# A pair's softmax inverses on one trip: one reciprocal, one transfer out, one back, and the multiplication moved in VectorE's order

## The chip, the cores and the metric

The kernel runs on one core of one Trainium2 chip. The metric is the device time of one execution in microseconds. Engines are named as in the profile: PE is TensorE (PEld its weight loads), DVE is VectorE, ACT is ScalarE, POOL is GpSimd, SP is SyncE. An engine with a `q` behind it (ACTq, SPq) is its queue as it issues a DMA.

## The reference, cut to what matters

The program computes two small transformer blocks over 512 tokens of width 1024. Two of its attentions are softmax attentions: `chunk_causal_softmax_attention` of the first block ("MLA", 8 heads) and `fox_attention` of the second ("fox", 16 heads, with a decay added to the scores).

```python
z = jnp.einsum("bhqd,bshd->bhqs", q_blk, k).astype(jnp.float32) * scale
p = jax.nn.softmax(jnp.where(allowed, z, -jnp.inf), axis=-1)
return jnp.einsum("bhqs,bshd->bhqd", p.astype(v.dtype), v)
```

The softmax divides by the sum of a query's exponentials. In MLA the output is also multiplied by a gate before its projection.

## The kernel before

All matrix products are of float32 operands split into a high and a low part, so each tile is three matmuls (lines 1171 to 1173) or, in attention, two or three (L1520, L1557). ScalarE writes the high part, VectorE subtracts it for the low part (`low`, L2704).

Both softmax attentions go over pairs of heads (4 in MLA, 8 in fox). Each pair has eight steps `s` = 0 to 7: four blocks of 128 queries of its first head, four of its second. The products of another unit of work (a projection) run beside it in eight shares. On every engine the order of a pair is written out by hand, as a string of a letter and a number, and the engines meet by semaphores alone: an instruction that waits holds everything behind it on its engine. Orders differ by kind and place: `_MLA` and `_MLA_LAST`; `_FOX` for pairs 0 to 5, `_NEAR` for pair 6, `_LAST` for pair 7.

- TensorE: `z` scores of a step (L1520 and a mask, L1531 or L1535), `t` transposes of its exponentials (L1544), `v` values of a head (L1556 to L1559), `g` and `a` a share of the products beside (`beside`). In pair 7 those shares are of the projection of the attention's outputs, and share k needs the low part of output k.
- ScalarE: `e` exponentials with their sum (L2197), `p` high part of the transposed (L2227), `r` one half of the output out of its bank (L2204), `s` and `y` staging of the next queries, keys and values, `w` high parts of the weights to come, `o` high part of an output (L2134), `d` the DMA of a head's four inverses per partition to a row in HBM (L2211), `b` and `f` the DMA of that row back to the 64 partitions of the head's half of `sq` (L2219).
- VectorE: `m` maximum of a step (L3075), `p` low part of the transposed, `n` reciprocal of a head's sums (L3080), `g` and `h` sum of an output's two parts (L2924), `k` the multiplication of the pair before by its inverses (`norm`, L3087, and in MLA the gate, L3091), `c` low parts of the weights to come (L2656), `s`, `y`, `o` the low parts of staging and outputs, `x` the products beside out of their banks (L2914).
- SyncE issues, in order, the weight loads (each waits for the `c3` that frees its slot) and in fox the copies of the staged heads to the other half of the partitions (`copy_halves`, L1086 and L1092).

Per pair there are four transfers of inverses: `d0`, `b0` in its middle, `d1` at its end, and `f1` for its second head in the next pair. `k0` of the next pair multiplies. After the last pair `norm` and the last output's parts stand behind everything.

Of the kernel before, what the change touches and what calls it, by code (L numbers as in the profile page):

```python
# [229 lines left out]
def hybrid_block_kernel(nc, ins, out):  # L230
# [4 lines left out]
    with ctx:  # L235
# [224 lines left out]
        PE_MLA = "z0 g0 z1 g1 z2 t0 z3 t1 z4 g2 t2 z5 t3 z6 g3 v0 t4 z7 g4 t5 t6 g5 t7 g6 g7 v1"  # L460
        ACT_MLA = "e0 e1 y1 p0 e2 p1 f1 w0 e3 p2 p3 s2 w1 d0 e4 e5 p4 y2 e6 b0 p5 e7 p6 r0 p7 s3 d1 r1"
        DVE_MLA = "m0 m1 m2 m3 p0 p1 p2 m4 p3 n0 m5 c0 c1 c2 y1 m6 p4 k0 c3 m7 p5 s2 p6 n1 g0 p7 y2 x0 x1 s3 g1"
        PE_FOX = "z0 g0 z1 g1 z2 t0 t1 z3 g2 z4 t2 g3 z5 t3 g4 z6 t4 t5 z7 v0 g5 t6 t7 g6 g7 v1"
        ACT_FOX = "w0 y0 e0 e1 w1 p0 e2 f1 s2 p1 e3 p2 p3 e4 e5 d0 y1 e6 s3 p4 p5 b0 e7 r0 p6 p7 d1 r1"
        DVE_FOX = "m0 m1 c0 m2 c1 p0 m3 s2 p1 m4 m5 p2 p3 n0 y0 m6 k0 c2 m7 c3 y1 p4 p5 g0 n1 p6 p7 x0 x1 s3 g1"


        PE_NEAR = "z0 z1 z2 g0 g1 t0 t1 z3 g2 z4 t2 z5 g3 t3 z6 g4 t4 t5 v0 g5 z7 g6 g7 t6 t7 a0 v1"
        ACT_NEAR = "y0 e0 e1 p0 p1 f1 e2 w0 w1 e3 p2 p3 e4 d0 e5 e6 o0 o1 p4 p5 b0 y1 r0 e7 p6 p7 s2 d1 r1"
        DVE_NEAR = "m0 m1 m2 m3 p0 y0 c0 c1 p1 p2 m4 m5 p3 n0 m6 k0 c2 c3 o0 o1 p4 y1 m7 p5 g0 x0 x1 n1 p6 p7 s2"  # L470


        PE_LAST = "z0 z1 z2 g1 t0 z3 t1 g2 t2 t3 z4 z5 z6 g3 t4 z7 g4 v0 t5 g5 t6 t7 g6 v1"
        ACT_LAST = "e0 s1 p0 e1 f1 y0 e2 o2 e3 p1 o3 w0 p2 y1 o4 p3 e4 o5 d0 w1 e5 o6 e6 e7 b0 p4 p5 d1 r0 p6 p7 b1 r1"
        DVE_LAST = "m0 m1 m2 h1 p0 m3 s1 o2 y0 p1 o3 c0 p2 m4 o4 k0 y1 p3 n0 o5 m5 c1 m6 m7 c2 n1 c3 p4 p5 o6 g0 p6 p7 g1"

        ACT_MLA_LAST = "e0 e1 y1 p0 e2 p1 f1 w0 e3 p2 p3 w1 d0 e4 e5 p4 o0 e6 b0 p5 o1 e7 p6 r0 d1 p7 o2 b1 r1"
        DVE_MLA_LAST = "m0 m1 m2 m3 p0 p1 p2 m4 p3 n0 m5 c0 c1 c2 y1 m6 p4 k0 c3 m7 p5 o0 n1 p6 g0 o1 p7 x0 x1 o2 g1"
        EARLY_OUT = {"mla": 3, "fox": 7}
# [59 lines left out]

        def inverse_half(hh):  # L540

            return sq[hh * HD:(hh + 1) * HD, 0, :]

        def low_rows(hh):
            return sq[hh * HD:(hh + 1) * HD, 1, :]

        def heads_before(kind, h):
            return h + (MLA_HEADS if kind == "fox" else 0)

        def pair_sums(pair, hh):  # L550
            return row_sums[:, pair % 2, hh, :]
# [1318 lines left out]
        def _(act):  # L1870
# [320 lines left out]
            def softmax_attention(kind, heads):  # L2191
# [13 lines left out]

                def inverse_to_row(i, hh):
                    h = heads_before(kind, 2 * i + hh)
                    act.wait_ge(A["sum_inverse"], 2 * i + hh + 1)
                    if h > 1:
                        act.wait_ge(inverse_back, 16 * (h - 1))  # L2210
                    nc.scalar.dma_start(inverse_rows[hh, :].rearrange("(p j) -> p j", p=P), pair_sums(i, hh))\  # L2211
                        .then_inc(inverse_out, 16)

                def inverse_to_half(i, hh):
                    h = heads_before(kind, 2 * i + hh)
                    act.wait_ge(inverse_out, 16 * (h + 1))
# [12 lines left out]
                def pair_of_heads(pair, order, here, ahead):  # L2229
                    for what, s in steps(order):  # L2230
# [402 lines left out]
        def _(dve):  # L2633
# [436 lines left out]
            def softmax_attention(kind, heads):  # L3070
# [45 lines left out]
                def pair_of_heads(pair, order, here, ahead):  # L3116
                    for what, s in steps(order):
# [638 lines left out]
```

## Time and profile before

| | |
|---|---|
| time, median of 3 runs | 1708.14 us (1707.88 to 1708.19) |
| profiled execution | 1708.22 us, span 1706.3 us, mean granted clock 0.996 |
| TensorE busy | 1676.5 us, 98% |
| VectorE busy | 1285.8 us, 75% |
| ScalarE busy | 952.9 us, 56% |
| MLA attention | from about 297 to 380 us |
| fox attention | from about 512 to 676 us |

The span runs from the first to the last instruction of the core. Busy times overlap between engines. As TensorE is nearly always busy, the time is its work and the holes in it; an idle time elsewhere costs nothing by itself. A matmul is pipelined, so its successor can start before its end, and a hole is best read from the starts.

### The profile page before, as it was taken

Reading aid. Unit: us, or ns where it says so; the run is one execution under the profiler, and the core shown is the slowest. Engines: PE = TensorE matmul, PEld = TensorE weight load, DVE = VectorE, ACT = ScalarE, POOL = GpSimd, SP = SyncE. Lnnn points to the kernel's source line nnn. Section 1 sums busy time; section 2 is a strip of 40 time slices with the busy share of each in tenths; the row PEclk is TensorE's granted clock in tenths of the full one; section 3 lists DMA queues with packets and bytes.
Section 4 is the critical chain, followed back from the end, with each engine's and each line's share of the span. In section 5 each row is a group of like instructions: output and inputs, shape, how many; then the busy total and the mean of one; then the engine's idle time right before and its main releaser. Section 6 shows DMA issues by size and latency. Waiting matters only on the chain.

```text
span 1706.3 us, 25098 instructions
## 1 busy us (share of the span) xinstructions
PE 1676.5 (98%) x9279; PEld 1441.0 (84%) x9279; DVE 1285.8 (75%) x2054; ACT 952.9 (56%) x1717; POOL 169.7 (10%) x147
## 2 busy tenths in 40 slices
PE   9999999999999998999999999999999999999998
PEld 7888877878788886789899998878887999999977
DVE  6378877776567887688798986785566979898966
ACT  4267875655436765477546364652235866464655
POOL 2011212000300000220000002420003000000041
PEclk9999999999999999999999999999999999999998
DMA  8222124224243333243233443313322432323621
GB/s 274 81 73 75 40 74 101 84 66 148 75 112 85 87 91 93 75 173 124 75 123 99 124 164 120 109 55 109 111 87 93 156 122 100 99 100 99 236 74 50
DMA packets 158163, 180.72 MB, mean 106 GB/s; under 512 B 22121, under 2 KB 130182, under 8 KB 156262
## 3 DMA queue, kind: packets, MB, share of 16 engines
q1 hardware_dynamic: 150790, 159.22, 30.1%
q10 hardware_dynamic: 7264, 20.05, 3.3%
q8 instruction: 69, 1.13, 0.3%
q14 instruction: 40, 0.33, 0.1%
HBM read 161.96 MB, written 12.63 MB: 102 GB/s over the span
## 4 chain that ended last, share of the span: by engine, by line
PE 82%; DVE 10%; ACT 3%; DMA 2%; issue 2%; POOL 1%; ACTq 0%; DVEq 0%; POOLq 0%; SPq 0%
PE bank L1171 24%; PE bank L1172 24%; PE bank L1173 24%; DMA raw_weights<-in_w_mlp_down 2%; DVE split_weights L2704 2%; PE bank L1520 2%; PE bank L1544 1%; PE bank L1439 1%; POOL ssum L3666 1%; DVE act_b L2704 1%; DVE split_weights L2656 1%; PE bank L1428 1%; DVE work L3087 1%; DVE act_a L2706 1%; PE bank L1557 1%
## 5 line engine op out<-in xcount | busy, mean ns | idle before, releaser
L1171 PE MATMUL bank<-act_a,split_weights 128*128 128x512 f32 (+1 forms) x1360 | 526.0, 387 | 7.5 <-DVE act_a L2704 3.7
L1173 PE MATMUL bank<-act_a,split_weights 128*128 128x512 f32 (+1 forms) x1360 | 519.0, 382 | 0.0
L1172 PE MATMUL bank<-act_a,split_weights 128*128 128x512 f32 (+1 forms) x1360 | 518.6, 381 | 0.0
L1171 PEld LDWEIGHTS bank<-act_a,split_weights 128*128 128x128 f32 x1360 | 256.2, 188 | 60.2 <-issue 6.1
L1173 PEld LDWEIGHTS bank<-act_a,split_weights 128*128 128x128 f32 x1360 | 255.9, 188 | 50.5
L1172 PEld LDWEIGHTS bank<-act_a,split_weights 128*128 128x128 f32 x1360 | 256.3, 188 | 45.2 <-issue 0.2
L1171 PE MATMUL bank<-act_b,split_weights 128*128 128x256 f32 (+1 forms) x648 | 207.3, 320 | 1.2 <-DVE split_weights L3398 1.2
L1173 PE MATMUL bank<-act_b,split_weights 128*128 128x256 f32 (+1 forms) x648 | 206.4, 319 | 0.0
L1172 PE MATMUL bank<-act_b,split_weights 128*128 128x256 f32 (+1 forms) x648 | 206.3, 318 | 0.0
L2646 DVE TENSOR_TENSOR split_weights<-raw_weights,split_weights 128x2048 fp32r<-128x2048 f32 x55 | 127.8, 2323 | 75.2 <-ACT split_weights L1882 62.4
L1882 ACT ACTIVATE split_weights<-raw_weights 128x2048 fp32r<-128x2048 f32 x51 | 97.3, 1908 | 118.4 <-PE bank L1173 118.4
L1171 PEld LDWEIGHTS bank<-act_b,split_weights 128*128 128x128 f32 x648 | 123.2, 190 | 10.7 <-DVE split_weights L3398 1.6
L1172 PEld LDWEIGHTS bank<-act_b,split_weights 128*128 128x128 f32 x648 | 123.2, 190 | 9.0 <-issue 0.5
L1173 PEld LDWEIGHTS bank<-act_b,split_weights 128*128 128x128 f32 x648 | 123.2, 190 | 8.4
L2402 ACT ACTIVATE split_weights<-sums 128x512 fp32r<-128x512 f32 x144 | 86.4, 622 | 62.5 <-DVE sums L3337 42.8
L1924 ACT ACTIVATE sq<-work 128x512 f32<-128x512 f32 x100 | 61.4, 624 | 85.9 <-DVE work L3278 45.5
L2402 ACT ACTIVATE split_weights<-raw_weights 128x512 fp32r<-128x512 f32 x108 | 63.6, 622 | 72.0 <-PE bank L1173 41.6
L3666 POOL TENSOR_TENSOR ssum<-ssum,sq 128x512 f32<-128x512 f32 x67 | 92.3, 1377 | 102.0 <-ACT sq L1924 97.7
L2704 DVE TENSOR_TENSOR split_weights<-sums,split_weights 128x512 fp32r<-128x512 f32 x144 | 96.5, 684 | 1.8 <-ACT split_weights L2402 0.6
L2704 DVE TENSOR_TENSOR act_b<-tmp,act_b 128x256 fp32r<-128x256 f32 (+3 forms) x168 | 84.7, 543 | 2.2 <-ACT act_b L878 1.3
L2704 DVE TENSOR_TENSOR split_weights<-raw_weights,split_weights 128x512 fp32r<-128x512 f32 (+1 forms) x111 | 75.3, 690 | 11.1 <-ACT split_weights L2402 11.1
L3670 POOL TENSOR_TENSOR ssum<-sq 128x512 f32<-128x512 f32 x14 | 20.9, 1491 | 597.2 <-ACT sq L1924 595.7
(357 smaller groups left out, 3221.8 us busy)
## 6 DMA issues: line engine op xcount, KB each, us to landing
raw_weights<-in_w_mlp_up SPq DMA_DIRECT2D x32, 1024.0 KB, 5.3
raw_weights<-in_w_mlp_down SPq DMA_DIRECT2D x32, 1024.0 KB, 5.3
raw_weights<-in_w_in SPq DMA_DIRECT2D x18, 1024.0 KB, 5.2
raw_weights<-in_w_conv_in SPq DMA_DIRECT2D x12, 1024.0 KB, 5.2
raw_weights<-in_w_attn_in SPq DMA_DIRECT2D x16, 512.0 KB, 5.2
raw_weights<-in_w_ple_gate SPq DMA_DIRECT2D x8, 1024.0 KB, 5.1
raw_weights<-in_w_out SPq DMA_DIRECT2D x4, 1024.0 KB, 5.4
raw_weights<-in_w_attn_in SPq DMA_DIRECT2D x4, 1024.0 KB, 5.3
```

What stands on the lines that cost most here:

```text
L1171: nc.tensor.matmul(dst, w[0], a[0], start=first, stop=False)
L1172: nc.tensor.matmul(dst, w[0], a[1], start=False, stop=False)
L1173: mm = nc.tensor.matmul(dst, w[1], a[0], start=False, stop=last)
L1428: mm = nc.tensor.matmul(banks[kt][:, c:S], qk(part)[:, kt * P:(kt + 1) * P], qk(0)[:, c:S], start=part == 2, stop=part == 3)
L1520: return nc.tensor.matmul(dst, qk(a)[0:rows, j * P:(j + 1) * P], qk(b)[0:rows, 0:cols], start=first, stop=last)
L1882: nc.scalar.activation(wsp[:, pl.wslot, 0, :], raw[:, pl.slot, :], ACT.Copy)\
L1924: nc.scalar.activation(sq[:, parity, :], src, ACT.Square).then_inc(sq_done, 1)
L2402: nc.scalar.activation(by_blocks(product_weights(pl, i, 0)), product_source(pl, j, i), ACT.Copy)\
L2646: V.tensor_tensor(wsp[:, pl.wslot, 1, :], raw[:, pl.slot, :], wsp[:, pl.wslot, 0, :].bitcast(F32), ALU.subtract).then_inc(w_split, 1)
L2704: V.tensor_tensor(dst, src, hi.bitcast(F32), ALU.subtract).then_inc(sem_, 1)
L3666: nc.gpsimd.tensor_tensor(ssum[:, :], ssum[:, :], sq[:, parity, :], ALU.add).then_inc(sq_added, 1)
L3670: nc.gpsimd.tensor_tensor(ssum[:, :], sq[:, 0, :], sq[:, 1, :], ALU.add).then_inc(sq_added, 2)
```

## The change

A pair's sums of both heads are inverted by one reciprocal over 128x8, sent to two rows by one DMA and brought back to all 128 partitions by one. `n0`, `d0`, `b0` and `f1` go. `n1` waits for all eight exponentials, `d1` for it; `b1` stands at the very end of ScalarE's order of each pair, and waits for `d1` to have landed. `k0` moves forward in VectorE's orders: in MLA from behind `p4` to behind `p1`, in fox from behind `m6` to behind `m4`, in pair 6 from behind `m6` to behind `m2`, in pair 7 from behind `o4` to behind `m7`. In pairs 6 and 7 more is moved: output 2's parts go from pair 7 into pair 6, the exponentials come sooner, outputs and staging later, and `c1` to `c3` of VectorE go behind `p7`. TensorE's orders are unchanged.

```diff
@@ -458,24 +458,24 @@
 
 
         PE_MLA = "z0 g0 z1 g1 z2 t0 z3 t1 z4 g2 t2 z5 t3 z6 g3 v0 t4 z7 g4 t5 t6 g5 t7 g6 g7 v1"
-        ACT_MLA = "e0 e1 y1 p0 e2 p1 f1 w0 e3 p2 p3 s2 w1 d0 e4 e5 p4 y2 e6 b0 p5 e7 p6 r0 p7 s3 d1 r1"
-        DVE_MLA = "m0 m1 m2 m3 p0 p1 p2 m4 p3 n0 m5 c0 c1 c2 y1 m6 p4 k0 c3 m7 p5 s2 p6 n1 g0 p7 y2 x0 x1 s3 g1"
+        ACT_MLA = "e0 e1 y1 p0 e2 p1 w0 e3 p2 p3 s2 w1 e4 e5 p4 y2 e6 p5 e7 p6 r0 p7 d1 s3 r1 b1"
+        DVE_MLA = "m0 m1 m2 m3 p0 p1 k0 p2 m4 p3 m5 c0 c1 c2 y1 m6 p4 m7 c3 p5 s2 n1 p6 g0 p7 y2 x0 x1 s3 g1"
         PE_FOX = "z0 g0 z1 g1 z2 t0 t1 z3 g2 z4 t2 g3 z5 t3 g4 z6 t4 t5 z7 v0 g5 t6 t7 g6 g7 v1"
-        ACT_FOX = "w0 y0 e0 e1 w1 p0 e2 f1 s2 p1 e3 p2 p3 e4 e5 d0 y1 e6 s3 p4 p5 b0 e7 r0 p6 p7 d1 r1"
-        DVE_FOX = "m0 m1 c0 m2 c1 p0 m3 s2 p1 m4 m5 p2 p3 n0 y0 m6 k0 c2 m7 c3 y1 p4 p5 g0 n1 p6 p7 x0 x1 s3 g1"
+        ACT_FOX = "w0 y0 e0 e1 w1 p0 e2 s2 p1 e3 p2 p3 e4 e5 y1 e6 s3 p4 p5 e7 r0 d1 p6 p7 r1 b1"
+        DVE_FOX = "m0 m1 c0 m2 c1 p0 m3 s2 p1 m4 k0 m5 p2 p3 y0 m6 c2 m7 c3 p4 p5 y1 n1 g0 p6 p7 x0 x1 s3 g1"
 
 
         PE_NEAR = "z0 z1 z2 g0 g1 t0 t1 z3 g2 z4 t2 z5 g3 t3 z6 g4 t4 t5 v0 g5 z7 g6 g7 t6 t7 a0 v1"
-        ACT_NEAR = "y0 e0 e1 p0 p1 f1 e2 w0 w1 e3 p2 p3 e4 d0 e5 e6 o0 o1 p4 p5 b0 y1 r0 e7 p6 p7 s2 d1 r1"
-        DVE_NEAR = "m0 m1 m2 m3 p0 y0 c0 c1 p1 p2 m4 m5 p3 n0 m6 k0 c2 c3 o0 o1 p4 y1 m7 p5 g0 x0 x1 n1 p6 p7 s2"
+        ACT_NEAR = "y0 e0 e1 p0 p1 e2 w0 w1 e3 p2 p3 e4 e5 e6 o0 o1 p4 p5 y1 r0 e7 o2 p6 p7 d1 s2 r1 b1"
+        DVE_NEAR = "m0 m1 m2 k0 m3 p0 y0 c0 c1 p1 p2 m4 m5 p3 m6 c2 c3 o0 o1 p4 y1 m7 p5 g0 x0 x1 n1 p6 p7 s2 o2"
 
 
         PE_LAST = "z0 z1 z2 g1 t0 z3 t1 g2 t2 t3 z4 z5 z6 g3 t4 z7 g4 v0 t5 g5 t6 t7 g6 v1"
-        ACT_LAST = "e0 s1 p0 e1 f1 y0 e2 o2 e3 p1 o3 w0 p2 y1 o4 p3 e4 o5 d0 w1 e5 o6 e6 e7 b0 p4 p5 d1 r0 p6 p7 b1 r1"
-        DVE_LAST = "m0 m1 m2 h1 p0 m3 s1 o2 y0 p1 o3 c0 p2 m4 o4 k0 y1 p3 n0 o5 m5 c1 m6 m7 c2 n1 c3 p4 p5 o6 g0 p6 p7 g1"
-
-        ACT_MLA_LAST = "e0 e1 y1 p0 e2 p1 f1 w0 e3 p2 p3 w1 d0 e4 e5 p4 o0 e6 b0 p5 o1 e7 p6 r0 d1 p7 o2 b1 r1"
-        DVE_MLA_LAST = "m0 m1 m2 m3 p0 p1 p2 m4 p3 n0 m5 c0 c1 c2 y1 m6 p4 k0 c3 m7 p5 o0 n1 p6 g0 o1 p7 x0 x1 o2 g1"
+        ACT_LAST = "e0 e1 s1 p0 e2 p1 e3 p2 o3 p3 e4 y0 o4 e5 w0 e6 o5 e7 p4 p5 o6 d1 r0 y1 p6 p7 w1 b1 r1"
+        DVE_LAST = "m0 m1 m2 h1 s1 m3 p0 p1 m4 o3 m5 p2 p3 o4 m6 y0 m7 k0 o5 p4 p5 n1 o6 y1 c0 g0 p6 p7 c1 c2 c3 g1"
+
+        ACT_MLA_LAST = "e0 e1 y1 p0 e2 p1 w0 e3 p2 p3 w1 e4 e5 p4 o0 e6 p5 e7 o1 p6 r0 p7 d1 o2 r1 b1"
+        DVE_MLA_LAST = "m0 m1 m2 m3 p0 p1 k0 p2 m4 p3 m5 c0 c1 c2 y1 m6 p4 m7 c3 p5 o0 n1 p6 g0 o1 p7 x0 x1 o2 g1"
         EARLY_OUT = {"mla": 3, "fox": 7}
 
 
@@ -537,15 +537,14 @@
 
             return slice(hh * HD, (hh + 1) * HD), slice((1 - hh) * HD, (2 - hh) * HD)
 
-        def inverse_half(hh):
-
-            return sq[hh * HD:(hh + 1) * HD, 0, :]
-
         def low_rows(hh):
             return sq[hh * HD:(hh + 1) * HD, 1, :]
 
         def heads_before(kind, h):
             return h + (MLA_HEADS if kind == "fox" else 0)
+
+        def pairs_before(kind, i):
+            return i + (MLA_HEADS // 2 if kind == "fox" else 0)
 
         def pair_sums(pair, hh):
             return row_sums[:, pair % 2, hh, :]
@@ -2203,20 +2202,19 @@
                     act.wait_ge(A["out"], FREE + h + 1)
                     nc.scalar.activation(low_rows(hh), banks[5][HD:2 * HD, :], ACT.Copy).then_inc(parts_copied, 1)
 
-                def inverse_to_row(i, hh):
-                    h = heads_before(kind, 2 * i + hh)
-                    act.wait_ge(A["sum_inverse"], 2 * i + hh + 1)
-                    if h > 1:
-                        act.wait_ge(inverse_back, 16 * (h - 1))
-                    nc.scalar.dma_start(inverse_rows[hh, :].rearrange("(p j) -> p j", p=P), pair_sums(i, hh))\
-                        .then_inc(inverse_out, 16)
-
-                def inverse_to_half(i, hh):
-                    h = heads_before(kind, 2 * i + hh)
-                    act.wait_ge(inverse_out, 16 * (h + 1))
+                def inverses_to_rows(i):
+                    p = pairs_before(kind, i)
+                    act.wait_ge(A["sum_inverse"], i + 1)
+                    if p:
+                        act.wait_ge(inverse_back, 16 * p)
+                    nc.scalar.dma_start(inverse_rows.rearrange("h (p j) -> p h j", p=P), row_sums[:, i % 2, :, :]).then_inc(inverse_out, 16)
+
+                def inverses_to_halves(i):
+                    p = pairs_before(kind, i)
+                    act.wait_ge(inverse_out, 16 * (p + 1))
                     if i:
                         act.wait_ge(A["gated"], i)
-                    nc.scalar.dma_start(inverse_half(hh), inverse_rows[hh, :].partition_broadcast(HD)).then_inc(inverse_back, 16)
+                    nc.scalar.dma_start(sq[:, 0, :], inverse_rows[:, None, :].to_broadcast((2, HD, S))).then_inc(inverse_back, 16)
 
                 def turned_hi(i, s):
                     hh, j = divmod(s, TT)
@@ -2243,12 +2241,9 @@
                         elif what == "r":
                             low_out(pair, s)
                         elif what == "d":
-                            inverse_to_row(pair, s)
+                            inverses_to_rows(pair)
                         elif what == "b":
-                            inverse_to_half(pair, s)
-                        elif what == "f":
-                            if pair:
-                                inverse_to_half(pair - 1, s)
+                            inverses_to_halves(pair)
                         elif what == "e":
                             exponentials(pair, s)
                         else:
@@ -3075,13 +3070,14 @@
                     V.reduce_max(negmax[:, s:s + 1], score_bank(s)[:, 0:(s % TT + 1) * P], AX, negate=True)\
                         .then_inc(A["negmax"], 1)
 
-                def inverse(i, hh):
-                    dve.wait_ge(A["exp"], 8 * i + TT * hh + TT)
-                    V.reciprocal(pair_sums(i, hh), pair_sums(i, hh)).then_inc(A["sum_inverse"], 1)
+                def inverse(i):
+                    dve.wait_ge(A["exp"], 8 * i + 8)
+                    both = row_sums[:, i % 2, :, :]
+                    V.reciprocal(both, both).then_inc(A["sum_inverse"], 1)
 
                 def norm(i):
                     out_ = output_tile(kind, i)
-                    dve.wait_ge(inverse_back, 16 * heads_before(kind, 2 * i + 2))
+                    dve.wait_ge(inverse_back, 16 * pairs_before(kind, i + 1))
                     dve.wait_ge(A["gathered"], FREE + 2 * i + 2)
                     by_tiles = out_.rearrange("p (j q) -> p j q", j=TT)
                     V.tensor_tensor(by_tiles, by_tiles, sq[:, 0, :].rearrange("p (q j) -> p j q", j=TT), ALU.mult)\
@@ -3132,7 +3128,7 @@
                         elif what == "m":
                             maxima(pair, s)
                         elif what == "n":
-                            inverse(pair, s)
+                            inverse(pair)
                         elif what == "k":
                             if pair:
                                 norm(pair - 1)
```

## Rows read from the trace of the kernel before

**Rows 1.** The page: busy time, share of the span, instructions
```profile
PE 1676.5 (98%) x9279; PEld 1441.0 (84%) x9279; DVE 1285.8 (75%) x2054; ACT 952.9 (56%) x1717; POOL 169.7 (10%) x147
```

**Rows 2.** Waits of TensorE, 280 to 720 us: us, times, longest us
```profile
PE bank L1544 <- ACT tmp L2197: 4.1, 5, 1.2
...
PE bank L1544 <- DVE act_b L2704: 3.3, 6, 0.9
```

**Rows 3.** Timeline of TensorE, MLA pair 2: start us, us, ... [idle before <-releaser]
```profile
352.64 0.39 PE L1172 MATMUL bank<-act_a,split_weights 128*128 128x512 f32 x1
352.87 0.40 PE L1173 MATMUL bank<-act_a,split_weights 128*128 128x512 f32 x1
354.24 0.66 PE L1544 MATMUL bank<-consts,tmp 128*128 128x128 f32 x4 [0.98 <-ACT tmp L2197]
```

**Rows 4.** Timeline of VectorE, MLA pair 2 (p2, k0, m7)
```profile
345.60 0.56 DVE L2704 TENSOR_TENSOR act_b<-bank,act_b 128x384 fp32r<-128x384 f32 x1 [1.63 <-ACT act_b L2227]
...
350.37 1.07 DVE L3087 TENSOR_TENSOR work<-work,sq 128x512 f32<-128x512 f32 x1
...
352.70 0.68 DVE L3075 TENSOR_REDUCE negmax<-bank 128x1 f32<-128x512 f32 x1
```

**Rows 5.** Timeline of VectorE, fox pair 3 (m5, k0, p4 with p5)
```profile
580.25 0.42 DVE L3075 TENSOR_REDUCE negmax<-bank 128x1 f32<-128x256 f32 x1 [0.71 <-PE bank L1531]
...
582.98 1.07 DVE L3087 TENSOR_TENSOR work<-work,sq 128x512 f32<-128x512 f32 x1
...
586.11 0.61 DVE L2704 TENSOR_TENSOR act_b<-bank,act_b 128x128 fp32r<-128x128 f32 x2
```

**Rows 6.** Busy by stretch (then PEclk, DMA share, GB/s): fox pairs 0, 3; pair 7
```profile
522.76:531.78 9.02, 9.02 (x51) 7.26 (x50) 7.46 (x17) 5.35 (x14) 0.00 (x0) 1.00 0.56 133
...
581.88:591.38 9.50, 9.01 (x51) 7.19 (x50) 8.29 (x18) 5.41 (x14) 0.00 (x0) 1.00 0.53 142
...
659.60:662.40 2.80, 2.74 (x7) 2.05 (x8) 1.97 (x5) 1.38 (x2) 0.00 (x0) 0.50 0.02 6
```

**Rows 7.** Timeline of TensorE, fox pair 3 (t0, t1), pairs 6 and 7, end
```profile
575.41 0.50 PE L1544 MATMUL bank<-consts,tmp 128*128 128x128 f32 x3
...
643.17 0.44 PE L1544 MATMUL bank<-consts,tmp 128*128 128x128 f32 x2 [0.51 <-ACT tmp L2197]
...
659.66 0.79 PE L1171 MATMUL bank<-act_a,split_weights 128*128 128x512 f32 x1 [1.97 <-DVE act_a L2704]
...
683.13 0.51 PE L1171 MATMUL bank<-act_a,split_weights 128*128 128x512 f32 x1 [1.73 <-DVE act_a L2704]
```

**Rows 8.** Timeline of ScalarE: e0 of MLA pair 2; d1, r1, e7 of fox
```profile
339.53 0.37 ACT L2197 ACTIVATE tmp<-bank,negmax 128x128 f32<-128x128 f32 x1 [1.14 <-DVE negmax L3075]
...
587.84 0.33 ACTq L2211 DMA_DIRECT2D inverse_rows<-row_sums  x1
591.58 0.59 ACT L2204 ACTIVATE sq<-bank 64x512 f32<-64x512 f32 x1 [3.45 <-PE bank L1557]
...
605.92 0.69 ACT L2197 ACTIVATE tmp<-bank,negmax 128x512 f32<-128x512 f32 x1 [0.54 <-DMA inverse_rows<-row_sums]
```

**Rows 9.** DMA issues, us to landing: d1 of fox pairs 0 and 5; d0; last b1
```profile
inverse_rows<-row_sums ACTq DMA_DIRECT2D x1, 2.0 KB, 5.7
...
inverse_rows<-row_sums ACTq DMA_DIRECT2D x1, 2.0 KB, 6.1
...
inverse_rows<-row_sums ACTq DMA_DIRECT2D x1, 2.0 KB, 1.4
...
sq<-inverse_rows ACTq DMA_DIRECT2D x1, 128.0 KB, 6.0
```

**Rows 10.** Timeline of SyncE: a weight load after c3, the last copy
```profile
585.92 1.00 SPq L895 DMA_DIRECT2D raw_weights<-in_w_attn_in  x2
...
655.97 0.66 SPq L1092 DMA_DIRECT2D act_b<-act_b  x1
```

**Rows 11.** Timeline of VectorE, the last multiplication
```profile
680.62 1.07 DVE L3087 TENSOR_TENSOR work<-work,sq 128x512 f32<-128x512 f32 x1 [2.82 <-DMA sq<-inverse_rows]
```

## The prediction

> **What bounds the kernel.** I began with the page. TensorE is busy for 1676.5 us of the 1706.3 us span [rows 1], so only holes in its stream can be won, some 30 us in all. The list of waits of TensorE alone, over the stretch of both softmax attentions, shows which holes there are: transposes that wait for an exponential five times, and for VectorE's low parts six times [rows 2]; and twice products wait for the low part of an output, in the last fox pair and behind it. The timelines then say what the late engine was doing.
>
> *MLA, pairs 1 to 3.* The last matmul of share g5 starts at 352.87 and t7 at 354.24 [rows 3]. Matmuls of this kind start 0.23 apart (352.64, 352.87), so the hole is 1.14 us. t7 waits for e7, e7 for m7, and m7 started at 352.70 [rows 4] because VectorE had the two multiplications of k0 in front of it (350.37, some 1.72 us to the next operation). Before p2 VectorE had stood still for 1.63 us [rows 4].
>
> *Fox, pairs 1 to 5.* VectorE does k0 at 582.98 and so brings p4 only at 586.11 [rows 5]; t6 waits for it. Pair 0 has no k0, and there the same stretch, from z6 to the next pair's z0, takes 9.02 us against 9.50 [rows 6].
>
> *Pairs 6 and 7.* In pair 6, t5 starts 0.51 late, since ScalarE stood at d0 waiting for n0. In pair 7, g2 waits 1.97 us for output 2, and after the pair the product of output 7 waits 1.73 [rows 7]; between them t6 waits 0.9, the longest of its kind [rows 2]. Behind the first of these waits the granted clock is 0.50 for 2.8 us [rows 6], which is 1.2 GHz where it was 2.4; before it fell TensorE had stood waiting.
>
> **The change, part by part.**
>
> *Four issues become two, two reciprocals one.* The second reciprocal goes, 12 times over. No row shows one over 128x8; it costs between one and two of the old ones, and neither decides. The issues on ScalarE's queue mostly lie beside its work. Where one has to wait, they don't: at 605.92 an exponential stood 0.54 behind b0's wait for d0 [rows 8]. d0 and b0 vanish from the middle of the pair, and with d0 the wait in pair 6. t5 would then start when e5 ends. e5 follows e4 directly and is over before t4. **Gain 0.7** (0.51 and the 0.2 by which a matmul's end overlaps its successor).
>
> *k0 moves forward in MLA.* After p1 there are 1.63 us of nothing [rows 4], k0 needs 1.72 and the old p2 starts where k0 will end. m7 then follows p4, at about 350.3, and no longer 352.7. e7 comes after p5 in the new ScalarE order. p5 waits for t5 (351.2) and ends about 351.8, e7 about 352.6. t7 wants to start at 353.10. The hole goes in all three pairs: 1.14, 1.14 and (its idle is 1.2, the longest of its kind [rows 2], against 0.98) 1.33: **gain 3.6**. What is late next: p7's low part ends 1 us ahead of v1. k0 itself needs the inverses back: b1 is issued after r1 (0.7 into the pair), lands in some 3 us, and k0 stands at 6.3. That fits.
>
> *k0 moves forward in fox.* It goes behind m4, where VectorE idled 0.71 [rows 5] waiting for z5. It overhangs by 0.3, which the idle time ahead of p3 and m6 takes up. m6 stays where the scores put it, then c2, m7, c3, p4: p4 can be done when ScalarE has turned it, about 0.9 earlier. Then t7's exponential e7 is the last to arrive, as it is in pair 0, so the whole effect is pair 0's: 9.50 less 9.02, five times: **gain 2.4**.
>
> *The wait at b1.* This is the new risk. b1 now stands behind r1 at the pair's end and waits for d1 to land. Everything of the next pair on ScalarE is queued behind it: in fox w0, y0, e0, e1, and t0 and t1 wait for these. d1 lands late in the six fox pairs whose products still load weights beside it: 5.7, 5.2, 5.4, 4.6, 5.3 and 6.1 us from issue, where the d0 of a quiet moment needs 1.4 [rows 9]. It is issued at 587.84 [rows 8], into the weight load that c3 sets free at 585.92 [rows 10]. Two readings. If d1 keeps its own duration, it lands 1.0 to 1.2 earlier, as it is issued earlier. If it lands when the burst of loads and copies has drained, it moves with c3: 1.05 earlier in pairs 1 to 5, and not at all in pair 0, but the 128 KB of b0 are out of that burst too, about 0.35. I take the second. The landings so moved, plus 0.5 for an issue that nothing hides [rows 8], stand against the end of r1 (592.17 in pair 3 [rows 8], earlier by the 0.48 gained): ScalarE would be late by 1.6, 0.85, 0.7, 0, 1.0 and 1.7. e1's sum ends about 0.6 ahead of t1 (they start at 575.41, 3.9 into the pair [rows 7]). So TensorE waits 1.0, 0.2, 0.1, 0 and 0.4 at t1 of pairs 1 to 5. In pair 6, where nothing is split ahead of e0, the lateness is within what e0 has. **Loss 1.7.** The other ends: 0 (first reading, short landing), and 6 if the transfer of twice as many 16-byte pieces lands 1 us later than that. In MLA e0 has 1.14 of idle ahead of it [rows 8], so the wait costs nothing.
>
> The Trainium skill bears on the two readings (DMA: Bandwidth & Descriptors, Queues, rings and completion order): a completion's semaphore write lands only after every earlier write of that DMA engine, across its queues. By that rule the second reading holds and the sum stays as here. By the first reading it would be about 1 us better. The trace leans to the rule, as d1 takes 1.4 alone and 4.6 to 5.7 beside a load.
>
> *The last pair.* The new orders put o2 into pair 6, one exponential after another, and c1 to c3 behind p7. Stalls of before: t1 0.5, g2 2.2, the lower clock 1.4 (half of 2.8), t6 1.1, v1 0.15, output 7 1.9 (each wait with the 0.15 to 0.2 of overlap that goes with it). Together 7.3 of the stretch from 653.37 to 683.13. I went through the three orders with the old durations, counting from z0. t1 and g2 start on time. t3 waits 0.2 for e3. z4 now wants its operands at 5.9, much earlier than before. Their copy was issued at 655.97 [rows 10], 2.6 after z0, and will be issued 0.7 later, since s1 comes after e1; landing in about 3 us, it costs 0.3. o3, o4 and o5 are each within 0.3 of g3, g4 and g5. p7 is ready at 16.5, v1 wants 16.1. c3 ends at 18.6 and the first product after v1 wants it at 17.9. Output 7: the multiplication at 680.62 had waited 2.82 for the inverses [rows 11], as b1 took 6.0 to land beside a load [rows 9]. That load is freed by c3 and now comes behind b1. The inverses land at 19.5, output 7 is split at 22, and TensorE asks at 23.5. So output 7 no longer delays. New stalls about 1.0, old ones 7.3: **gain 6.3**. Bounds: 7.3 if nothing new arises, 2 if a new hole at z4 or at c3 is like that of g2 and the clock falls again.
>
> **Sum.** 3.6 + 2.4 + 0.7 + 6.3 - 1.7 = 11.3 us. The profiled execution took 1708.22 with a span of 1706.3; the median is 1708.14, so what is taken off the one may be taken off the other: 1708.1 - 11.3 = 1696.8. After each attention the products run on without a hole, and what follows them is set by TensorE, so I see nothing that gives the time back.
>
> **Rivals.**
>
> 1. *ScalarE's wait at b1 takes the place of the waits removed.* For it: the landings [rows 9]. Against: 0.6 of slack at t1, and the burst moves too. If each of the six fox pairs loses 1.2 at its start in place of 0.3, the sum is 11.3 - 5.4: 1702.2. Chance 0.17.
> 2. *The last pair brings little*: z4 or c3 stalls and the clock falls. Gain 2 there: 1701.1. Chance 0.10.
> 3. *Everything fits*, no wait at b1, last pair without a new stall: 11.3 + 1.7 + 1.0 = 14.0: 1694.1. Chance 0.10.
> 4. *No effect*: another engine's chain is as long, and the holes reappear elsewhere. Against it speaks pair 0, which shows the gain where k0 is absent. 1706 to 1708. Chance 0.04.
> 5. *Slower*: the paired transfer of 256 pieces lands behind everything that SyncE queues, and ScalarE stands at b1 in every one of the ten boundaries. Slower by over 0.2% needs 14.7 us of loss more than I count, 1.5 per boundary, thus a landing 2.1 us later than I take (1.5 and the 0.6 of slack). At 2.5 later it is 1712. Its place is e0 behind b1. Chance 0.04.
>
> My own case has 0.55. The range: the forecast's own width is 1694.5 to 1699.5; to hold 8 in 10 it takes in rival 3 and most of 1 and 2: 1693 to 1702.5. About 0.2%, 3.4 us, is what a measurement of this kernel can tell from no change. Faster: my case, rivals 1 to 3, 0.92; same 0.04; slower 0.04.
>
> **What would show it.** In the waits of TensorE, no transposes waiting for an exponential in MLA, and the z6-to-z0 stretch of fox at 9.0 in every pair. Right for the loss: on ScalarE, w0 after r1 with an idle put down to the transfer of row sums, and transposes 3.9 us into the pair waiting for an exponential. In the last pair, a granted clock at its full level and some 23.5 us from z0 to output 7's product. The prediction is wrong if fox pairs get longer, if the multiplication waits for its inverses in its new place, or if TensorE stands at z4 or behind c3 for more than 1 us.

## The result and the profile after

The changed kernel takes 1719.81 us (median of 4 runs, 1716.67 to 1722.22) against 1708.01 (4 runs, 1707.33 to 1708.19) on the same chip: ratio 1.0070, 95% interval 1.0054 to 1.0086. It is slower by 11.8 us, where I had forecast 11.3 us less than before. The profiled execution took 1720.47 us with a span of 1718.6.

The page of the kernel after, its first lines and (with lines left out) the chain that ended last, by line:

```profile
span 1718.6 us, 25041 instructions
## 1 busy us (share of the span) xinstructions
PE 1681.0 (98%) x9279; PEld 1444.2 (84%) x9279; DVE 1286.1 (75%) x2042; ACT 951.4 (55%) x1717; POOL 169.9 (10%) x147
...
PE bank L1170 23%; PE bank L1171 22%; PE bank L1172 22%; DMA sq<-inverse_rows 4%; DVE split_weights L2699 2%; DMA raw_weights<-in_w_mlp_down 2%; PE bank L1519 1%; PE bank L1438 1%; DVE act_b L2699 1%; POOL ssum L3662 1%; PE bank L1543 1%; DMA inverse_rows<-row_sums 1%; PE bank L1556 1%; PE bank L1427 1%; DVE act_a L2701 1%
```

TensorE has the 9279 matmuls of before [rows 1]. New on the chain is `sq<-inverse_rows`, the one transfer back, with 4% of the span; eight of the twelve transfers are on it, each counted whole, 7.0 to 9.6 us from issue to use. The waits from 280 to 740 us say who stood for it (engine, tile, line, releaser: us in total, times, longest):

```profile
DVE work L3083 <- DMA sq<-inverse_rows: 21.1, 8, 5.8
...
PE bank L1556 <- DVE act_b L2699: 4.6, 4, 1.6
...
PE bank L1170 <- DVE act_a L2699: 3.7, 1, 3.7
ACT split_weights L1890 <- DMA inverse_rows<-row_sums: 3.1, 3, 1.3
PE bank L1543 <- DVE act_b L2699: 2.9, 1, 2.9
PE bank L1519 <- DMA act_b<-act_b: 2.8, 1, 2.8
...
PE bank L1170 <- DVE act_b L2699: 2.2, 1, 2.2
```

L3083 is the multiplication k0. It waits eight times, 21.1 us. The transposes that waited in [rows 2] have only one large wait left, of 2.9, and that is a new one: a transpose in pair 6 that waits for the low part p0, which stands behind k0 and m3. The values (L1556) wait four times: v0 of MLA's pairs 1 to 3 for some 1 us each, for low parts that now stand behind a waiting k0, and v1 of the last fox pair for 1.6. The wait that I had put into the sum, ScalarE's for `d1` at b1, is there too and small (3.1 us, three times).

The timeline of MLA pair 2 shows the transfer's issue and the multiplication, and the windows what moved between them (us, busy by engine with its count, granted clock, DMA share, GB/s):

```profile
339.02 0.53 ACTq L2217 DMA_DIRECT2D sq<-inverse_rows  x1
...
346.52 1.08 DVE L3083 TENSOR_TENSOR work<-work,sq 128x512 f32<-128x512 f32 x1 [1.39 <-DMA sq<-inverse_rows]
```

```profile
340.00:341.00 1.00, 1.00 (x7) 0.87 (x7) 0.62 (x2) 0.31 (x2) 0.00 (x0) 1.00 0.06 10
341.00:342.00 1.00, 1.00 (x6) 0.81 (x5) 0.43 (x1) 0.63 (x5) 0.00 (x0) 1.00 0.13 51
342.00:343.00 1.00, 1.00 (x7) 0.91 (x6) 0.03 (x1) 0.39 (x2) 0.00 (x0) 1.00 0.13 51
343.00:344.00 1.00, 1.00 (x8) 0.82 (x7) 0.74 (x2) 0.71 (x2) 0.00 (x0) 1.00 0.13 51
344.00:345.00 1.00, 1.00 (x7) 0.86 (x7) 0.97 (x3) 1.00 (x4) 0.00 (x0) 1.00 0.13 51
345.00:346.00 1.00, 1.00 (x8) 0.83 (x7) 0.14 (x1) 1.00 (x3) 0.00 (x0) 1.00 0.15 55
```

The DMA engines are otherwise idle, yet the transfer moves 51 GB/s for five microseconds, at a DMA share of 0.13: two of 16 engines. Before the change a transfer for one head (128 KB, issued at 342.91) looked like this in the same windows:

```profile
344.00:345.00 1.00, 1.00 (x9) 0.86 (x7) 0.00 (x0) 1.00 (x3) 0.00 (x0) 1.00 0.51 111
345.00:346.00 1.00, 1.00 (x9) 0.81 (x8) 0.40 (x1) 0.64 (x4) 0.00 (x0) 1.00 0.06 21
```

The counts of packets, first after (340 to 346), then before (343.5 to 346), fit that:

```profile
DMA packets 131, 0.27 MB, mean 45 GB/s; under 512 B 2, under 2 KB 2, under 8 KB 130
```

```profile
DMA packets 80, 0.13 MB, mean 52 GB/s; under 512 B 16, under 2 KB 16, under 8 KB 80
```

Beside the 2 KB pieces (128 and 64; the first also has one packet of another queue) there are 2 small packets after and 16 before. In the experiments below the two transfers of a pair have 32 small packets together with 64 x 512, 4 with 2 x 32 x 512 and 8 with 4 x 16 x 512. So I read it that not the doubled size cost most, but that 14 engines stood by. The source of the new transfer is 2 x 64 x 512 (head, repetition, query), that of the old one 64 x 512.

Where TensorE's time went I read from the ends of the values matmuls (v0 and v1) in the timelines, kernel after against kernel before. The table gives what each stretch adds, in us, to the time of the kernel before; the two right-hand columns are experiments told below (the last is the kernel whose pair 6 issues its transfers first):

| stretch, up to the end of | forecast | after | two halves | last edit but one |
|---|---|---|---|---|
| MLA pair 0, v1 | 0 | +1.1 | +1.0 | +0.1 |
| MLA pair 3, v1 | -3.6 | -0.6 | -4.4 | -4.3 |
| fox pair 0, v1 (MLA's last k0 in it) | 0 | +3.8 | +0.6 | +0.5 |
| fox pair 5, v1 | -0.7 | -1.1 | -0.5 | -2.4 |
| fox pair 6, v1 | -0.7 | +4.0 | -0.7 | -0.7 |
| fox pair 7, v1, then the span's end | -6.3 | +0.5, +4.5 | -3.0, -1.3 | -4.2, -1.2 |
| sum | -11.3 | +12.3 | -8.3 | -12.3 |

The first row is not the change's: TensorE is already 1.2, 1.0 and 0.1 us behind the kernel before some 8 us into these executions, and stays so until the attentions. So up to 1 us of a sum is the start of that one execution.

The losses of the kernel after lie where k0 stands close behind the transfer: the end of MLA, pair 6, and the last output. MLA's pairs 1 to 3 belong to them too. There t7's wait is gone, and from v0 to v1 each is 1.2 to 1.4 us shorter, but v0 comes 0.95 to 1.25 later in each, which leaves 0.6 of the gain in all. The timelines of VectorE and TensorE at these places:

```profile
388.00 1.07 DVE L3083 TENSOR_TENSOR work<-work,sq 128x512 f32<-128x512 f32 x1 [5.76 <-DMA sq<-inverse_rows]
...
642.45 1.06 DVE L3083 TENSOR_TENSOR work<-work,sq 128x512 f32<-128x512 f32 x1 [4.68 <-DMA sq<-inverse_rows]
...
690.89 1.06 DVE L3083 TENSOR_TENSOR work<-work,sq 128x512 f32<-128x512 f32 x1 [5.27 <-DMA sq<-inverse_rows]
```

```profile
644.46 0.52 PE L1543 MATMUL bank<-consts,tmp 128*128 128x128 f32 x3 [2.94 <-DVE act_b L2699]
...
669.66 0.77 PE L1519 MATMUL bank<-act_b 128*128 128x256 f32 x2 [2.79 <-DMA act_b<-act_b]
...
693.39 0.80 PE L1170 MATMUL bank<-act_a,split_weights 128*128 128x512 f32 x1 [3.67 <-DVE act_a L2699]
```

The last k0 waits 5.27 where it had waited 2.82 [rows 11], and output 7's product waits 3.67 where it had waited 1.73 [rows 7]. The scores z4 of pair 7 wait 2.79 for a copy of 256 KB that has nothing to do with the inverses. It is issued at 663.92; the windows show why it is late:

```profile
663.00:664.00 1.00, 1.00 (x8) 0.59 (x7) 0.97 (x2) 0.97 (x3) 0.00 (x0) 1.00 0.14 53
664.00:665.00 1.00, 1.00 (x8) 0.86 (x8) 1.00 (x3) 0.97 (x4) 0.00 (x0) 1.00 0.13 49
665.00:666.00 1.00, 0.94 (x6) 0.50 (x5) 0.97 (x3) 0.78 (x3) 0.00 (x0) 1.00 0.77 195
666.00:667.00 1.00, 0.87 (x7) 0.52 (x5) 0.01 (x1) 0.79 (x4) 0.00 (x0) 1.00 0.54 119
667.00:668.00 1.00, 0.00 (x0) 0.00 (x0) 0.00 (x0) 0.87 (x2) 0.00 (x0) 1.00 0.13 51
668.00:669.00 1.00, 0.00 (x0) 0.00 (x0) 0.00 (x0) 0.00 (x0) 0.00 (x0) 1.00 0.08 29
```

The copy's bulk moves from 665 to 667 on all engines, and a rest drains until 669 at 51 GB/s again: I read it as its share on the two engines that still have the slow transfer in front; with the slow transfer gone (first experiment) the delay is gone too. TensorE stands from 667. Behind this wait, behind that of pair 6 and behind that for output 7 the granted clock is at half, 1.2 GHz, three times in all:

```profile
645.70:649.00 3.30, 3.30 (x12) 2.81 (x11) 1.47 (x5) 0.57 (x2) 0.00 (x0) 0.50 0.02 5
...
669.66:672.66 3.00, 3.00 (x11) 2.90 (x12) 1.98 (x5) 1.66 (x7) 0.00 (x0) 0.50 0.00 0
...
693.39:696.50 3.11, 3.11 (x7) 2.48 (x8) 2.94 (x5) 1.31 (x3) 0.00 (x0) 0.50 0.01 5
```

### The profile page after: what moved, and what is told of

Its sections match the earlier page's. It is cut to its first block, busy times and chain, and to the rows that moved or that the text cites. A ratio compares the mean times of both kernels' runs of the same rounds, so it can differ in the third digit from the quotient of the medians.

```text
span 1718.6 us, 25041 instructions
## 1 busy us (share of the span) xinstructions
PE 1681.0 (98%) x9279; PEld 1444.2 (84%) x9279; DVE 1286.1 (75%) x2042; ACT 951.4 (55%) x1717; POOL 169.9 (10%) x147
## 4 chain that ended last, share of the span: by engine, by line
PE 76%; DVE 10%; DMA 7%; ACT 3%; issue 2%; POOL 1%; DVEq 0%; POOLq 0%; ACTq 0%; SPq 0%
PE bank L1170 23%; PE bank L1171 22%; PE bank L1172 22%; DMA sq<-inverse_rows 4%; DVE split_weights L2699 2%; DMA raw_weights<-in_w_mlp_down 2%; PE bank L1519 1%; PE bank L1438 1%; DVE act_b L2699 1%; POOL ssum L3662 1%; PE bank L1543 1%; DMA inverse_rows<-row_sums 1%; PE bank L1556 1%; PE bank L1427 1%; DVE act_a L2701 1%
```

## Experiments

### Two transfers back in place of the one

```diff
-nc.scalar.dma_start(sq[:, 0, :], inverse_rows[:, None, :].to_broadcast((2, HD, S)))
+for hh in range(2):
+    nc.scalar.dma_start(sq[hh * HD:(hh + 1) * HD, 0, :], inverse_rows[hh, :].partition_broadcast(HD))
```

> The changed kernel, with one part undone: a pair's inverses are spread back by two transfers of 64 partitions (one for each head) at b1's place, not by one of 128; everything else as changed. Theory A (the one transfer's shape: its source goes over the two heads first, and the trace shows it moving 256 KB in 5.3 us at 50 GB/s on a DMA share of 0.12, two of 16 engines): each half lands about 3 us after its issue as the halves did before the change, k0 and g of the next pair wait for nothing, the 21.1 us of VectorE's waits for it go to under 3, and the time is 1694 to 1702 us. Theory B (256 KB asked for at one place is slow in whatever shape): landing stays at 5 to 6.6 us and the time at 1715 to 1721. Theory C (ScalarE's wait for d1's landing at b1, and the new orders of the pairs, cost it, not the transfer): the time stays over 1710 though the halves land in 3 us.

Measured: 1699.85 us (5 runs, 1699.64 to 1701.39), ratio to before 0.9954 (0.9941 to 0.9968). From the changed kernel this one edit takes 20 us. The waits of the same stretch:

```profile
DVE work L3084 <- DMA sq<-inverse_rows: 4.5, 3, 2.3
...
PE bank L1556 <- DVE act_b L2700: 1.6, 1, 1.6
```

and the windows behind the issue at 337.47 (both halves):

```profile
338.00:339.00 1.00, 1.00 (x6) 0.79 (x5) 0.88 (x3) 0.00 (x1) 0.00 (x0) 1.00 0.14 49
339.00:340.00 1.00, 1.00 (x7) 0.89 (x6) 0.54 (x2) 0.48 (x3) 0.00 (x0) 1.00 0.51 184
340.00:341.00 1.00, 1.00 (x6) 0.85 (x5) 0.00 (x0) 0.85 (x3) 0.00 (x0) 1.00 0.08 29
```

The same 256 KB are through in some 2 us. Theories B and C fall. VectorE still waits 4.5 us, more than the 3 that theory A allowed: 2.3 of them at MLA's end.

### The same two transfers, of another shape

```diff
-inverse_rows[hh, :].partition_broadcast(HD)
+inverse_rows[hh, None, None, :].to_broadcast((2, HD // 2, S))
```

The addresses, pieces and bytes are the same; only the list of dimensions is another. In the second kernel here the 2 stands as 4 (and `HD // 4`).

> As the kernel with two half transfers, but each half's source is written as 2 x 32 x 512 over the same addresses, in place of 64 x 512: the same bytes, pieces, number of transfers and moment. Theory A: each half then moves on two engines again; 128 KB at the 50 GB/s that the trace of the changed kernel shows are 2.6 us each, so 4 us from issue to landing for the first, and 6 to 7 for the second if they share the two engines (time 1712 to 1721), or 4.5 if they don't (1697 to 1706). Theory B (bytes at one place) and theory C (waits of ScalarE, orders): no difference from the plain two halves, within 1 us.

> As the kernel with two half transfers, but each half's source is written as 4 x 16 x 512 over the same addresses. Theory A (as many engines as the outermost dimension counts; two carried 50 GB/s): four carry 100 GB/s at a DMA share of 0.25, the two halves take 2.6 us together and the second lands 4 us after its issue, 1 us more than with 64 x 512; with VectorE's waits at k0 between those of the two kernels (4.5 and 38.1 us) the time is 1701 to 1708. Theory B (any shape but 64 x 512 is as slow as 2 x 32 x 512): 1740.

Measured: 1743.52 us with 2 x 32 (4 runs, 1739.56 to 1743.70; ratio 1.0200, 1.0184 to 1.0215), and 1705.19 with 4 x 16 (10 runs, 1702.84 to 1706.09; 0.9978, 0.9968 to 0.9987). The windows, first 2 x 32 (issued at 341.75, multiplied at 350.15), then 4 x 16 (issued at 337.00):

```profile
343.00:350.00 7.00, 7.00 (x43) 6.18 (x42) 2.65 (x7) 5.00 (x14) 0.00 (x0) 1.00 0.11 39
```

```profile
338.00:339.00 1.00, 1.00 (x7) 0.89 (x6) 0.61 (x2) 0.32 (x2) 0.00 (x0) 1.00 0.18 63
339.00:340.00 1.00, 1.00 (x6) 0.79 (x5) 0.42 (x1) 0.63 (x5) 0.00 (x0) 1.00 0.25 68
340.00:341.00 1.00, 1.00 (x7) 0.92 (x6) 0.04 (x1) 0.38 (x2) 0.00 (x0) 1.00 0.23 84
```

DMA shares of 0.11 to 0.13 (two of 16) and 0.25 (four of 16) go with outermost dimensions of 2 and 4. Both halves of the first kernel take the same two engines one after the other, else the share would be 0.25. The first kernel is 22 us above the top of my range. They move 39 GB/s on the mean, not 50, and VectorE waits 38.1 us for them, 11 times. The granted clock is also at half in six stretches, 27 us together, where the kernel after has three with 10 us and the one with 64 x 512 has none in the attentions. With 4 x 16 the time is in its range, though the rate, 63 to 84 GB/s, is below the 100 expected. This settles the cause: not the bytes, nor the number of transfers.

### The shape alone, in the kernel before

```diff
+src = inverse_rows[hh, None, None, :].to_broadcast((2, HD // 2, S)) if hh else inverse_rows[hh, :].partition_broadcast(HD)
```

> The kernel before the change, with its second half transfer alone (head 1 of a pair) written as 2 x 32 x 512 over the same addresses. Only its landing is measured here. Theory A: it moves at 50 GB/s, so that 128 KB take 2.6 us and land 3.9 to 4.2 us after the issue, against 3.0; a DMA share of 0.12 while it runs; the time 1708 to 1711, since k0 comes 4 us and more behind it in most pairs. Theory B: it lands in 3.0 us as before.

Measured: 1711.62 us, one execution. The second half is issued at 343.64 and moves from 345 to 348:

```profile
345.00:348.00 3.00, 2.93 (x19) 2.47 (x18) 1.38 (x4) 2.63 (x7) 0.00 (x0) 1.00 0.12 46
```

Some 4.3 us from issue to the end of its data, where before it had landed after 3.0: as theory A has it. The time is 3.5 above the median before and 0.6 above the range. In the positions fox pairs 1 to 6, where k0 is far behind, lose nothing, MLA's end adds 1.2 and the end of the span 2.8.

### The slow transfer kept, k0 back at its old place

```diff
-DVE_MLA = "m0 m1 m2 m3 p0 p1 k0 p2 m4 p3 m5 c0 c1 c2 y1 m6 p4 m7 c3 ...
+DVE_MLA = "m0 m1 m2 m3 p0 p1 p2 m4 p3 m5 c0 c1 c2 y1 m6 p4 k0 m7 c3 ...
```

and k0 behind `m6` in fox and pair 6.

> The changed kernel with its one slow transfer back, but with VectorE's multiplication k0 at its old place in all pairs but the last (behind p4 in MLA, behind m6 in fox and the pair before the last). Theory A (the slow transfer costs only where k0 stands and waits for it): k0 now comes 8 to 10 us behind the issue and waits for nothing inside MLA and fox, the old idle stretches of TensorE return (1.14 us three times in MLA, 0.49 us five times in fox), the wait at MLA's end (5.8 us) and in the last pair stay: 1708 to 1713, 7 to 12 faster than the changed kernel. Rival (the slow transfer hurts by itself, ScalarE's wait at b1 being what costs): 1716 to 1722.

Measured: 1716.56 us (5 runs, 1713.49 to 1717.26), ratio 1.0048 (1.0034 to 1.0061). That is 3 us under the changed kernel, not the 7 to 12 expected, and within the rival's numbers. The profiled execution was the lowest of the five. In it VectorE waits only twice for the transfer, 11.7 us: at MLA's end and behind pair 7. MLA's pairs gain 2.0 (0.6 in the kernel after) and pair 6 0.7 (it lost 4.0). So no wait for the transfer is left inside the pairs, as I had it; but MLA's end adds 5.1 and the end of the span 3.9, since nothing stands there between issue and multiplication, wherever k0 is in the orders. The 3 us between this execution and the median I can't place.

The old idle stretches of TensorE come back only in part, which I had not expected. From v0's end to v1's end the fox pairs 1 to 5 took 6.9 to 7.0 us before, take 6.4 to 6.5 in the kernel after and 6.5 to 6.65 here; MLA's pairs 1 to 3 took 9.8 to 10.0, then 8.6, and 9.3 to 9.55 here. So of the 0.48 that a fox pair gains, k0's new place brings some 0.1 on top of the other changes, and of the 1.2 to 1.4 of an MLA pair 0.7 to 0.9. The rest came with what else the diff changed in these orders: `n0`, `d0` and `b0` gone, in MLA `m7` ahead of `c3`, in fox `y1` behind `p5`. No run separates these, nor shows k0's move alone.

### The last two pairs with their old orders

As the kernel with two half transfers, but `ACT_NEAR`, `ACT_LAST`, `DVE_NEAR`, `DVE_LAST` of before, without the steps that the joining removes:

```diff
-DVE_LAST = "m0 m1 m2 h1 s1 m3 p0 p1 m4 o3 m5 p2 p3 o4 m6 y0 m7 k0 o5 p4 p5 n1 o6 y1 c0 g0 p6 p7 c1 c2 c3 g1"
+DVE_LAST = "m0 m1 m2 h1 p0 m3 s1 o2 y0 p1 o3 c0 p2 m4 o4 k0 y1 p3 o5 m5 c1 m6 m7 c2 n1 c3 p4 p5 o6 g0 p6 p7 g1"
```

> As the kernel with two half transfers, but the orders of ScalarE and VectorE in the last two fox pairs are those of the kernel before (k0, products and outputs 2 to 6 at their old places; only d, b and n joined). It isolates what the new orders of the last two pairs bring. Theory A (the slow transfer ate the gain, the new orders bring what I had put down for them: 6.3 us in the last pair and 0.7 at t5 of pair 6): 5 to 8 us slower than the plain two halves, so 1700 to 1709. Theory D (the new order of the last pair brings nothing or costs): within 1 us of the plain two halves, or faster.

Measured: 1705.49 us (11 runs, 1704.15 to 1708.57), 5.6 more than the two halves on the same chip. The new orders of pairs 6 and 7 bring 5.6 us; I had put down 7.0. But 0.7 of these were never theirs: with the old orders pair 6 gains its 0.7 as well, since `d0` is gone here too. So the 5.6 stand against 6.3 for the last pair. With the old orders the granted clock is at half for 6.8 us in pair 7; with the new ones, and two halves, it stays full.

### Transfers back behind the next pair's e0 and e1

```diff
-ACT_FOX = "w0 y0 e0 e1 w1 p0 ... p6 p7 r1 b1"
+ACT_FOX = "w0 y0 e0 e1 f1 w1 p0 ... p6 p7 r1"
-ACT_NEAR = "y0 e0 e1 p0 p1 ...
+ACT_NEAR = "y0 e0 e1 f1 p0 p1 ...
```

`f1` issues both halves of the pair before. The kernel with two halves had still gained only 0.5 us in fox pairs 1 to 5 where k0's move shows 0.48 five times. ScalarE's timelines at the start of fox pair 2 tell why: two halves (first fence), and this kernel (second):

```profile
548.60 0.59 ACT L2203 ACTIVATE sq<-bank 64x512 f32<-64x512 f32 x1 [3.12 <-PE bank L1556]
...
549.77 1.10 ACTq L2218 DMA_DIRECT2D sq<-inverse_rows  x2
...
550.98 1.06 ACT L1890 ACTIVATE split_weights<-raw_weights 128x1024 fp32r<-128x1024 f32 x1 [1.78 <-issue]
```

```profile
548.09 0.59 ACT L2203 ACTIVATE sq<-bank 64x512 f32<-64x512 f32 x1 [3.12 <-PE bank L1556]
548.71 1.06 ACT L1890 ACTIVATE split_weights<-raw_weights 128x1024 fp32r<-128x1024 f32 x1
```

> As the kernel with two half transfers, but in the fox pairs the two transfers back are issued in the next pair behind its exponentials e0 and e1, not at the end of their own pair; MLA and the last fox pair stay. Theory C' (what is left of the shortfall in the fox pairs is ScalarE's stand at b1 plus two issues of 0.45 to 0.6 us ahead of w0, y0 and e0: the trace of the two halves has e0 3.8 us behind v1's end, against 2.1 before, and v1's end slips by 0.96, 0.76, 0.04 and 0.13 us at the four boundaries that follow): those slips go, 2 to 3 us faster than the two halves, 1697 to 1698. Rival (the slips come from k0's new place or from the multiplication by four row's wider forms on VectorE): within 0.7 us of the two halves, 1699 to 1701. If the transfers now land after k0's place, VectorE waits at k0 instead and the time is 1701 or more.

Measured: 1699.16 us (5 runs, 1698.70 to 1700.93), ratio 0.9948 (0.9935 to 0.9962), against 0.9954 for the two halves, which ran on another chip: the total tells nothing. The positions do: the four slips are gone, and fox pairs 1 to 5 gain 2.4 us. But pair 6 gives 0.8 back, where it had gained 0.7, because its k0 stands early, right behind `m2`:

```profile
631.79 1.10 DVE L3087 TENSOR_TENSOR work<-work,sq 128x512 f32<-128x512 f32 x1 [3.02 <-DMA sq<-inverse_rows]
```

### The last pair, pair 6 and MLA's end

Three edits, one upon the other:

```diff
-ACT_LAST = "... p4 p5 o6 d1 r0 y1 p6 p7 w1 b1 r1"
+ACT_LAST = "... p4 p5 o6 y1 d1 r0 p6 p7 w1 b1 r1"
-DVE_LAST = "... m7 k0 o5 p4 p5 n1 o6 y1 c0 g0 p6 p7 c1 c2 c3 g1"
+DVE_LAST = "... m7 k0 o5 c0 p4 p5 n1 o6 y1 g0 p6 p7 c1 c2 c3 g1"
...
-ACT_NEAR = "y0 e0 e1 f1 p0 p1 ...
+ACT_NEAR = "f1 y0 e0 e1 p0 p1 ...
...
-ACT_MLA_LAST = "... e7 o1 p6 r0 p7 d1 o2 r1 b1"
+ACT_MLA_LAST = "... e7 o1 d1 p6 r0 p7 o2 b1 r1"
```

> As the one before, and in the last fox pair y1 on ScalarE ahead of d1 and r0, c0 on VectorE ahead of p4, not behind y1. The trace of the two halves has v1 of the last pair waiting 1.56 us for VectorE's p7, behind idle stretches of 0.50 and 0.70 us on VectorE. Theory (these two idle stretches fill, p7 ends 0.9 us earlier and with it v1 and the output products): 0.6 to 1.0 us faster than the one before. Rival (the weight share c3 or k0 of the last pair ends the tail anyway): within 0.3 us of it.

> As the kernel with the transfers back behind e1 and the tuned last pair, but in the pair before the last (where k0 stands early, behind m2) the two transfers back are issued first, ahead of y0 and e0. The trace of the kernel before this one has VectorE waiting 3.0 us at that k0 and TensorE 1.3 us at a transposition behind it; v0's end slips there by 0.8 us, where with the transfers at the end of their own pair it gained 0.7. Theory (k0 stands ahead of the landing): 1.2 to 1.6 us faster, 1696.2 to 1696.6. Rival (the two issues of 1.1 us ahead of y0 and e0 cost there what they save at k0): within 0.4 us of 1697.8.

> As the one before, and in MLA's last pair d1 is issued ahead of p6 and b1 ahead of r1 on ScalarE. VectorE waits 2.15 us there for the transfers back before MLA's last multiplication, and the positions slip by 0.5 us between MLA's end and the first fox values. Theory: up to 0.5 us faster than the one before. Rival: the wait for d1's own landing (3.5 to 4.3 us in MLA) ends at the same place as r1's wait for v1, and nothing changes, within 0.3 us.

Measured, 5 runs each: 1697.83 us (ratio 0.9939, 0.9926 to 0.9953), then 1696.64 (0.9935, 0.9921 to 0.9948), then 1696.12 (0.9931, 0.9918 to 0.9945). The first brings 1.3 us, a little over what was expected, as v1's wait falls from 1.56 to 0.4. The second ran on another chip than the first. Against the kernel before on its own chip it is 0.7 better, with intervals that overlap, so the 1.2 to 1.6 expected rest on the positions: pair 6 gains 0.7 and no longer gives back 0.8, which is 1.5. The third is 0.5 less in the medians, as expected, but its runs (1695.85 to 1696.52) and those of the kernel ahead of it (1695.85 to 1697.14) overlap, and in the profiled executions the spans are 1694.2 and 1694.0; whether it does anything stays open. In the positions v1 of MLA's last pair comes 0.5 later and MLA's end gives back 0.3 less, which speaks against a gain. The last is 11.8 us faster than before and 23.7 faster than the changed kernel. The waits of TensorE from 280 to 740 us in it, the three longest lines:

```profile
PE bank L1170 <- ACT work L2182: 1.4, 2, 1.2
PE bank L1337 <- ACT sq L1923: 0.7, 1, 0.7
PE bank L1556 <- DVE act_b L2703: 0.7, 2, 0.4
```

The first two were there before the change, with the same numbers.

## Why the prediction was wrong

*The step that failed* is in the part on k0 in MLA: "`b1` is issued after `r1`, lands in some 3 us, and k0 stands at 6.3. That fits." The 3 us were those of a 64-partition transfer, put without a bound on one that no row of before showed. Measured, from the issue at 339.02 to the multiplication at 346.52, it was 7.5. k0 and the last output hung on it, and so it took the gains in MLA, in pair 6 and behind the last pair; in fox pairs 1 to 5 k0 stands late enough, waits 0.5 at most, and the gain stayed. Undone alone, it gives 20.0 us back. The five rivals missed it too: the slower one put the late landing on the way out (`d1`), and that lands in 4.4 us at the median, as it does with the two halves (4.3).

The Trainium skill has the rule (DMA: Bandwidth & Descriptors, Why a DMA increments its semaphore by 16 and not by 1): the number of DMA engines is the largest number up to 16 that divides the outermost dimension, other than 1, of both sides. It spoke against this change, and I did not apply it to the one new access pattern in the diff. By it, 128 partitions against an outermost 2 make two engines; the shares of 0.13, 0.12 and 0.25 at outermost dimensions of 2, 2 and 4 agree.

Point by point, with the transfer's shape mended:

- *k0 in MLA, 3.6*: the size is right. t7's wait is gone, and pairs 1 to 3 gain 4.4, MLA's end gives back 0.6, for a net 3.8. Of the 3.8 between v0 and v1, k0's place brings 2.4.
- *k0 in fox, 2.4*: the size is right, 0.44 to 0.51 between v0 and v1 in each of pairs 1 to 5, in the kernel after too. The cause is mostly another: with k0 at its old place 0.32 to 0.37 of it are still there. Pair 0, which I took for the proof, has no k0, but showed only what a pair gains at most.
- *Pair 6, 0.7*: right (0.7), and for the reason given, `d0`. Its early k0 brought nothing: with k0 at its old place pair 6 gains the same 0.7, in two kernels. With the slow transfer it cost 4.0, and with the transfers back behind e1 0.8.
- *Loss at b1, 1.7*: the size was right, the places were not, so part of it is luck: I had 1.0 at pair 1, which slips by nothing in either kernel. The kernel after slips by 0.7 and 0.6 at the starts of fox pairs 3 and 4, the two halves by 1.9 in all, most at pairs 2 and 3. There a second issue of 0.62 is in it too, and behind e1 both go.
- *The last pair, 6.3*: mis-sized. With two halves it brings 4.3 (3.0 to v1, 1.3 behind it). The largest piece missing is v1's wait of 1.56 for p7: I had p7 ready at 16.5 with v1 at 16.1. I had not found VectorE's two idle stretches ahead of p4 and of y1. Its old stalls were a little larger than I read, too: the clock of before stays at half until 663.04, so for 3.4 us and not the 2.8 of my window.
- *The last output*: "output 7 no longer delays" holds with the two halves and not with one transfer, where the product waits 3.67. But the inverses do not land at 19.5. With the two halves they land 22.5 us behind z0, as the second half takes 6.1 from its issue beside other loads. The product waits only 0.2 because TensorE asks for it at 25.4 and not at 23.5.
- *Readings*: `d1` beside a load took 4.6 to 6.1 us by the prediction's own list, not 4.6 to 5.7; and rival 5 counted by its own rule gives 1715.8 us for a landing 2.5 later (1.9 at ten boundaries), not 1712. Neither is in the sum.

The conditions I had named for being wrong (the multiplication waits in its new place; TensorE stands at z4) are what happened. With all of it mended the best kernel stands at 1696.1. That it is close to the forecast of 1696.8 confirms nothing, as it is reached in part by steps that the change does not have; the change with its transfer mended alone stands at 1699.85, 3 us short.

## What to carry to other kernels

When a diff joins transfers, write down the list of dimensions of both sides of the new one and look at the outermost: it set here how many DMA engines worked, and a landing time may be carried over only to a transfer of the same list. In the profile, a DMA share that sits at 0.13 or 0.25 for microseconds while all else is idle is that sign. And before a consumer is moved towards its producer, know the producer's duration with a bound: k0's new place gained at most 0.9 us in a pair, and cost TensorE up to 4.0 there.

## What the runs showed that I had not expected

- The list of dimensions over the same addresses decided a factor of three to four in rate: in one-microsecond windows 51 GB/s with an outermost 2, up to 84 with 4, up to 184 with 64.
- A transfer confined to two engines delays others: the copy issued at 663.92 was done for the most part at 667 and released z4 at 669.66, 5.7 us after its issue; with the two halves the same copy was issued at 652.72 and released z4 at 655.86, 3.1 after.
- Two transfers issued one behind the other on ScalarE's queue take it 1.04 to 1.20 us mostly, 1.6 to 2.6 four times, where a single one took 0.45 to 0.61. In fox, behind e1, they cost TensorE nothing; at the pair's end, ahead of e0 and behind the wait for `d1`, they did, and no run tells the two parts of that apart.
- A step that the diff makes in passing (`y1` behind `p5`) can bring more than the one that the change is named for: with k0 back at its old place two thirds of the gain in a fox pair were still there.
